# Nine jobs of the mixing product: both high terms in one matmul of 512 columns, gathered one unit later

## The reference, cut to what matters

```
u = rms_norm(h, mix_pre_gain)                       # 256 x 2048
p = u @ w_in                                        # 2048 x 5120
b_gate, c_gate, v_a, val_b, gate_b = split(p)       # 1024 columns each
y_a = b_gate * causal_dwconv(c_gate * v_a, conv_a_w)            # 3 taps
g   = causal_dwconv(val_b * sigmoid(gate_b), conv_b_w) + bias   # 31 taps
y_b = silu(layer_norm(g))
o   = concat(y_a, y_b) @ w_out
```

## Time and profile before

| | |
|---|---|
| median of three runs | 2030.54 us |
| the profiled execution | 2030.97 us, span 2028.8 us |
| TensorE busy | 2005.8 us, 99% of the span |
| VectorE busy | 1408.6 us, 69% |
| ScalarE busy | 1010.2 us, 50% |
| granted clock | 0.999 of full speed |

### The profile page before, as it was taken

How to read it: one execution, slowest core, us unless ns; L and a number is a source line. 1 busy time by engine, 2 the same in 40 slices (tenths; PEclk the granted TensorE clock), 3 DMA queues, 4 the chain that set the end, 5 groups by cost and what they waited for, 6 DMA issues and landing times.

```text
span 2028.8 us, 28149 instructions
## 1 busy us (share of the span) xinstructions
PE 2005.8 (99%) x11404; PEld 1759.0 (87%) x11404; DVE 1408.6 (69%) x1722; ACT 1010.2 (50%) x1340; POOL 8.0 (0%) x19
## 2 busy tenths in 40 slices
PE   7999999999999999999999999999999999999998
PEld 7999988888888888888888898888888888888887
DVE  6999967665555555565577766566577888888764
ACT  5767555544444444444455455445444545454543
POOL 0000000000000000000000000000000000000000
PEclk9999999999999999999999999999999999999999
DMA  8655564866656566665637665656565454545573
GB/s 272 187 181 171 182 223 133 275 218 187 196 184 199 186 190 197 186 198 187 195 96 230 188 215 193 227 187 214 187 193 182 151 171 150 173 154 178 171 264 105
DMA packets 305857, 384.24 MB, mean 189 GB/s; under 512 B 11673, under 2 KB 237209, under 8 KB 303936
## 3 DMA queue, kind: packets, MB, share of 16 engines
q1 hardware_dynamic: 305584, 382.38, 59.6%
q10 hardware_dynamic: 144, 0.07, 0.0%
HBM read 378.20 MB, written 4.19 MB: 188 GB/s over the span
## 4 chain that ended last, share of the span: by engine, by line
PE 96%; DMA 1%; DVE 1%; issue 1%; ACT 1%; SPq 0%; POOL 0%; ACTq 0%; POOLq 0%; DVEq 0%
PE job_banks L545 32%; PE job_banks L548 16%; PE job_banks L617 11%; PE job_banks L615 11%; PE job_banks L616 11%; PE job_banks L517 3%; PE job_banks L516 3%; PE job_banks L518 3%; PE aux_banks L787 2%; DMA raw_weights<-in_w_up 1%; PE aux_banks L652 1%; DMA resid<-in_x 1%; PE aux_banks L518 0%; PE aux_banks L517 0%; PE aux_banks L516 0%
## 5 line engine op out<-in xcount | busy, mean ns | idle before, releaser
L1275 DVE TENSOR_TENSOR weights_low<-raw_weights,weights_high 128x1024 fp32r<-128x1024 f32 x696 | 841.8, 1223 | 473.9 <-ACT weights_high L852 468.8
L852 ACT ACTIVATE weights_high<-raw_weights 128x1024 fp32r<-128x1024 f32 x696 | 728.0, 1056 | 605.8 <-PE job_banks L617 243.2
L545 PE MATMUL job_banks<-act_a,weights_high 128*128 128x512 f32 (+1 forms) x2008 | 590.3, 380 | 5.9 <-DVE act_a L1299 4.5
L548 PEld LDWEIGHTS job_banks<-act_a,weights_low 128*128 128x128 f32 x1880 | 347.5, 188 | 75.6
L548 PE MATMUL job_banks<-act_a,weights_low 128*128 128x256 f32 (+1 forms) x1880 | 368.7, 277 | 0.0
L545 PE MATMUL job_banks<-act_b,weights_high 128*128 128x512 f32 x1024 | 326.9, 400 | 0.0
L545 PEld LDWEIGHTS job_banks<-act_a,weights_high 128*128 128x128 f32 x2008 | 303.7, 190 | 7.5 <-issue 5.0
L615 PE MATMUL job_banks<-weights_high,act_b 128*128 128x512 f32 x736 | 287.1, 390 | 0.0
L617 PE MATMUL job_banks<-weights_high,act_b 128*128 128x512 f32 x736 | 286.4, 389 | 0.0
L616 PE MATMUL job_banks<-weights_low,act_b 128*128 128x512 f32 x736 | 286.4, 389 | 0.0
L548 PEld LDWEIGHTS job_banks<-act_b,weights_low 128*128 128x128 f32 x1024 | 192.3, 188 | 45.1
(11 more groups left out here) (146 smaller groups left out, 1683.3 us busy)
## 6 DMA issues: line engine op xcount, KB each, us to landing
raw_weights<-in_w_up SPq DMA_DIRECT2D x128, 512.0 KB, 3.8
raw_weights<-in_w_down SPq DMA_DIRECT2D x128, 512.0 KB, 4.3
raw_weights<-in_w_in_b SPq DMA_DIRECT2D x128, 512.0 KB, 4.1
raw_weights<-in_w_in SPq DMA_DIRECT2D x80, 512.0 KB, 3.9
raw_weights<-in_w_in_a SPq DMA_DIRECT2D x64, 512.0 KB, 4.7
raw_weights<-in_w_out SPq DMA_DIRECT2D x32, 512.0 KB, 4.4
raw_weights<-in_w_out_a SPq DMA_DIRECT2D x32, 512.0 KB, 4.4
raw_weights<-in_w_v SPq DMA_DIRECT2D x32, 512.0 KB, 4.4
```

The costliest lines, as they stand in the source:

```text
L545: made = e.matmul(o_both, wh[:, k, f * P:(f + 1) * P], rhs, start=opens, stop=False)
L548: made = e.matmul(o[:, 0, low_toks], wl[:, k, f * P:(f + 1) * P], x[:, first + kt, 0, low_toks], start=False, stop=kt == job.tiles - 1)
L852: e.activation(high[:, s, :], raw[:, r, :], ACT.Copy).then_inc(*high_done.inc(n))
L1275: e.tensor_tensor(low[:, s, :], raw[:, r, :], high[:, s, :].bitcast(F32), ALU.subtract).then_inc(*low_done.inc(n))
```

## The change

The first nine jobs of `mix_a` (c, v and b of the first three pairs of tiles) lose `direct` and become `apart`: their matmuls are those of `narrow_unit`, their part and value lie in `squares` (tiles 0 to 3 the parts, 4 to 7 the values, by pair). ScalarE copies the second halves when the job's last unit is used, as with other narrow jobs; its copy of c to `cvpad` (L992) goes, since VectorE's gather of c writes `cvpad` itself. VectorE gathers a job behind its step of the first unit of the job that follows. The product of c and v is made there too, that is behind the first unit of b instead of before it; the other taps of the short convolution start one unit later, and y is made and split behind the first unit of the next product's c, instead of before it. The last three jobs stay direct, with c times v and the taps moved in the same way; their y is made as before. The diff:

```diff
@@ Job
         self.direct = False
+        self.apart = False
@@ build: order, banks
-        for job in mix_b[2:] + mix_a + group_jobs:
+        for job in mix_b[2:] + mix_a[-3:] + group_jobs:
             job.direct = True
+        for job in mix_a[:-3]:
+            job.apart = True
@@
-            mix_a[3 * i].freed = [(kept, ("c", i))]
-            mix_a[3 * i + 1].freed = [(product, ("cv", i))]
-            mix_a[3 * i + 2].freed = [(product, ("y_a", i))]
+        mix_a[-3].freed = [(kept, "c")]
+        mix_a[-2].freed = [(product, ("cv", pairs - 1))]
+        mix_a[-1].freed = [(product, ("y_a", pairs - 1))]
@@
         def part_of(job):
+            if job.apart:
+                return squares[:, 2 * job.pair:2 * job.pair + 2, :]
             return partial[:, job.pair, :].rearrange("p (f n) -> p f n", f=2)
 
         def value_of(job):
+            if job.apart:
+                return squares[:, 2 * job.pair + 4:2 * job.pair + 6, :]
             return value[:, job.pair, :].rearrange("p (f n) -> p f n", f=2)
@@ scalar
+            def part_apart(job):
+                e.wait_ge(*unit_used.at(job.last))
+                if apart_free[job.pair] is not None:
+                    e.wait_ge(*gathered.at((apart_free[job.pair].id, 0)))
+                e.activation(part_of(job), pair_of(job)[:, :, TOKENS:2 * TOKENS], ACT.Copy).then_inc(
+                    *part_copied.inc(job.id))
+                apart_free[job.pair] = job
@@
+            def split_y_a(i):
+                e.wait_ge(*product.at(("y_a", i)))
+                split(("y_a", i), "b", slice(2 * i, 2 * i + 2), BOTH, conv3)
+
             for i in range(pairs):
                 c_job, v_job, b_job = mix_a[3 * i:3 * i + 3]
-                units_of(c_job)
-                there(e, c_job)
-                if i:
-                    e.wait_ge(*x_low.at(("y_a", i - 1)))
-                e.activation(cvpad[:, :, CONV_A - 1:], of_job(c_job), ACT.Copy).then_inc(*kept.inc(("c", i)))
+                for n in range(c_job.at, c_job.last + 1):
+                    freed(n)
+                    if n == c_job.at and i > 0:
+                        split_y_a(i - 1)
+                if c_job.apart:
+                    part_apart(c_job)
+                else:
+                    e.activation(cvpad[:, :, CONV_A - 1:], of_job(c_job), ACT.Copy).then_inc(*kept.inc("c"))
                 units_of(v_job)
+                if v_job.apart:
+                    part_apart(v_job)
                 for n in range(b_job.at, b_job.last + 1):
                     freed(n)
-                    if n == b_job.at:
+                    if n == b_job.at + 1:
                         e.wait_ge(*product.at(("cv", i)))
...
-                e.wait_ge(*product.at(("y_a", i)))
-                split(("y_a", i), "b", slice(2 * i, 2 * i + 2), BOTH, conv3)
+                if b_job.apart:
+                    part_apart(b_job)
+            split_y_a(pairs - 1)
@@ vector
+            def gather_apart(job, dst):
+                e.wait_ge(*part_copied.at(job.id))
+                e.tensor_tensor(dst, pair_of(job)[:, :, 0:TOKENS], part_of(job), ALU.add).then_inc(
+                    *gathered.inc((job.id, 0), (job.id, 1)))
+
+            def make_y_a(i):
+                b_job = mix_a[3 * i + 2]
+                if b_job.apart:
+                    gather_apart(b_job, value_of(b_job))
                 there(e, b_job)
...
+                for n in range(c_job.at, c_job.last + 1):
+                    freed(n)
+                    if n == c_job.at and i > 0:
+                        make_y_a(i - 1)
+                for n in range(v_job.at, v_job.last + 1):
+                    freed(n)
+                    if n == v_job.at and c_job.apart:
+                        gather_apart(c_job, c_values)
                 for n in range(b_job.at, b_job.last + 1):
                     if n < b_job.last or i < pairs - 1:
                         freed(n)
-                    if n == b_job.at + 1:
+                    if n == b_job.at:
+                        if v_job.apart:
+                            gather_apart(v_job, value_of(v_job))
+                        else:
+                            e.wait_ge(*kept.at("c"))
+                        there(e, v_job)
+                        e.tensor_tensor(c_values, c_values, of_job(v_job), ALU.mult).then_inc(
+                            *product.inc(("cv", i)))
+                    if n == b_job.at + 2:
                         convolve_a(i)
+            make_y_a(pairs - 1)
             freed(mix_a[-1].last)
```

More of the change, by code:

```diff
@@ L841, in scalar @@
             part_free = [None, None]
+            apart_free = [None, None]
             highs_made = 0
@@ L1460, in convolve_a @@
                                                ALU.mult, ALU.add).then_inc(*conv_a_done.inc((j, k)))
[L1462 to L1472, removed]
-                    if n == b_job.at + 1:
-                        convolve_a(i)
+            def gather_apart(job, dst):
[6 more added lines that the diff above has]
+                    gather_apart(b_job, value_of(b_job))
                 there(e, b_job)
@@ L1479, in vector @@
                 split(("y_a", i), "b", slice(2 * i, 2 * i + 2), BOTH, conv3)
+            for i in range(pairs):
+                c_job, v_job, b_job = mix_a[3 * i:3 * i + 3]
+                c_values = cvpad[:, :, CONV_A - 1:]
+                for n in range(c_job.at, c_job.last + 1):
[6 more added lines that the diff above has]
+                        gather_apart(c_job, c_values)
+                for n in range(b_job.at, b_job.last + 1):
+                    if n < b_job.last or i < pairs - 1:
+                        freed(n)
+                    if n == b_job.at:
[7 more added lines that the diff above has]
+                    if n == b_job.at + 2:
+                        convolve_a(i)
+            make_y_a(pairs - 1)
             freed(mix_a[-1].last)
```

## The result

Eight executions of the changed kernel have a median of 2036.84 us (2035.79 to 2038.57), eight of the kernel before beside them 2030.96 (2029.84 to 2032.10): a ratio of 1.003, 95% interval 1.002 to 1.004. It is slower by 5.9 us, 1.8 more than the 0.2% that can be told from no change. The same kernel timed once more on another chip, in eleven executions against 27, gave 2036.63 against 2031.71, 1.0023 (1.0013 to 1.0032): 4.9 us.

What follows compares the result with a forecast made beforehand. PE was taken as the bound, VectorE 5 to 10% behind; VectorE's gathers would make the stage's end 3.97 us late. The profiled 2030.97 plus 3.97 is 2034.9, so a median of 2034.5 us, range 2031.5 to 2037.3.

Steps and rivals of the forecast that it cites:

- PE saves 3.4 us: Over 36 units PE saves 0.094 us each, 3.4 us in all, with k tiles of 0.696 instead of 0.72.
- VectorE's delay: VectorE gets nine gathers, 2.02 us per product, and is 4.34 us late from its residual of unit 77 on.
- (1): First product: gathers cost 2.02 us, 0.27 gained, 0.3 added for y; delay 2.05 at VectorE's residual of unit 53.
- (2): Second product: gathers cost 2.02 us more, but waits of 1.75 around y and the next convolution go; delay 2.32.
- (3): Third product: gathers cost 2.02 us more; VectorE's delay is 4.34 from its residual of unit 77 on.
- The holds: PE waits for gathers before units 52, 60, 64 and 72: 0.6, 2.5, 2.4 and 1.3 us, together 6.9.
- a sign that it is wrong: Forecast wrong if PE never waits in the stage, unit 80 starts before 250, or PE's clock falls in a hold.
- The end of the stage: VectorE, 4.34 us later, meets PE: the square's mean at 256.94 (3.85 late), unit 83 at 262.98 (3.97 late).
- The sum: Profiled execution of 2030.97 plus 3.97 is 2034.9; it lies 0.43 above the median, so the forecast median is 2034.5 us.
- the likeliest case: The forecast case of 2034.5 us, chance 0.73, with its own range of 2032.5 to 2036.3.
- Hidden after all: Rival: VectorE's additions fall into its waits and PE keeps its 3.4 us, giving 2027.1; chance 0.07.
- The stall stays: Rival: ScalarE's wait for y at the second product costs VectorE its 1.75 us again, giving 2036.3; chance 0.16.

Runs made afterwards that it cites:

- eighteen additions out: Changed kernel with eighteen of VectorE's 512-column convolution additions cut to one column (part of the second branch left out): 2028.42 us, 0.9986.
- the old places: Changed kernel with gathers in the new form, but the product, y and ScalarE's splits where they stood before: 2036.84 us against 2030.80, 1.0029.

## Why the prediction was right

The direction and the mechanism hold: VectorE's gathers, not PE, set the end of the stage. Its steps in their order:

- **PE saves 3.4 us.** Right: 3.27 with eighteen additions out.
- **VectorE's delay.** (1) At low 53 it was put at 2.05 and is 1.55 (157.62 against 156.07): low 48 came 0.52 earlier, not 0.27, and the wait inside the first y stayed 0.77, where I had added 0.3. (2) At low 65 the forecast was 2.32, and it is 2.32: the second product cost 0.77 instead of 0.27, because it was this y whose wait grew, by 0.35, and because the stalls given back were priced too high: 0.23, 1.06 and 0.46 in brackets are 0.13, 1.13 and 0.35 from start to start, 1.61 instead of 1.75. (3) At low 77 4.34 was forecast, 4.39 measured. So that 2.32 was met to the digit is luck, two errors that cancel: 0.50 too much at the first product, 0.50 too little at the second.
- **The holds.** Forecast 0.6, 2.5, 2.4 and 1.3, measured 0.24, 2.26, 1.11 and 1.11. The first is smaller with the delay at low 53. The third is smaller for a cause that the prediction names as a sign that it is wrong, and that did come: the clock fell in a hold, the one before unit 60 (0.80 from 191 to 194 us, 0.63 from 194 to 197). So PE needed 12.94 us for units 60 to 63 (192.41 to 205.35) where four units of 2.786 make 11.14, and the clock's 0.6 + 1.1 = 1.7 is what it lacked. By the account above it cost the kernel nothing: unit 64 would have waited for the same gather that much longer. Unit 72 starts at 230.47, forecast 230.4.
- **The end of the stage.** The mean at 256.91 against a forecast 256.94. Unit 83 at 263.24 against 262.98: VectorE's residual of the last y is 4.60 later, not 4.34. Behind the moved residuals the product y stands directly behind the tap whose result it needs, 1.77 us after the taps' start instead of 1.58, where a residual used to stand between; that is 0.19 on top of the 4.41 by which the sums of squares are late (254.46 against 250.05). So this term is 4.23, not 3.97.
- **The sum.** 3.97 forecast; 4.23 at unit 83, 4.35 at 349, 5.9 and 4.9 in the two timings: 2036.84 is inside the range, and 0.5 above the end of the likeliest case's own. It is 2.3 above the forecast of 2034.5. The part that the forecast lacks is the clock's, about 1.4 us in the profiled execution, behind a wait that has not changed.
- **The chances.** "Hidden after all" is refuted by the kernel itself and by the additions taken out: it needs some nine to eighteen of them gone. "The stall stays" is refuted: low 64 waits for nothing. Its price was wrong too: with the stall back, at the old places, the time is 6.0 us above the kernel before on its chip, against 5.9 and 4.9 for the changed kernel, and VectorE's delay is the same.

Is the 1.4 us the change's doing? The eleven executions of the second timing speak to it. Four took 2034.93 to 2035.51 and six 2036.61 to 2037.29 (one, 2041.11, stands alone). The 27 of the kernel before on that chip split likewise: ten from 2030.01 to 2031.07, sixteen from 2031.31 to 2032.78. Group against group the change costs 2035.17 - 2030.49 = 4.7 us, or 2036.71 - 2031.86 = 4.9. The profiles go with it: a falling clock near 350 stands in the changed kernel's two profiles (2036.65 and 2036.66), none in that of the kernel before (2030.97); and the kernel before with GpSimd's additions, profiled in an execution of 2032.50, which lies in its upper group, has the fall there too, at a clock of 0.83 from 340 to 350 us. The changed kernel with GpSimd's additions (2035.28), which has the longest hold of all (3.37), shows a full clock behind the same wait. So the fall is not bound to the change, and holds ahead of it don't make it sure. In the first timing five of eight executions before lay in the lower group and one or none of the changed kernel's, which is why it shows 5.9. Whether the change makes the fall more frequent stays open: seven of eight and seven of eleven against three of eight and seventeen of 27 is too little to tell. The difference between group medians, 4.7 to 4.9, is still 0.4 above the 4.35 at 349 us; I have no line for that.

## What to carry to other kernels

A cheaper form of matmul that leaves its sum in two banks moves work from PE to whatever empties them: here 0.38 us of PE per job against 0.60 to 0.71 of VectorE. With VectorE 5 to 10% behind PE in that stage, three jobs fitted and nine did not; count per stage how many fit before changing them all. When the engine that frees the banks is itself the bound, freeing them sooner gives back only what it spares that engine, here 1.4 of 4.35 us. And sixteen additions moved from VectorE to GpSimd were no relief here: VectorE lost beside them what it had saved.

## What the runs showed of the hardware that was not expected

- GpSimd's addition of 512 columns takes 1.3 to 2.3 us by the profile, whose times on GpSimd are rough, and VectorE's taps beside it lose about as much as the additions taken from VectorE saved (7.4 against 7.7 us).
- A plain fp32 matmul of 256 columns takes 0.43 us, 3.6 times an fp32r matmul of that width in this kernel (0.12).
- Behind the same wait of 2.05 us near 345 to 349 the granted clock falls to 1.2 GHz in some profiles (the changed kernel, twice) and stays at 2.4 in others (the kernel before, the changed kernel with GpSimd's additions); a fall costs 1.4 to 1.6 us. That it differs between executions of one kernel is inferred from the two groups of times, not seen in two profiles of one kernel. A fall in the stretch that VectorE bounds moved unit 72 by nothing (230.47, forecast 230.4).
